# Moved steps around the latent statistics and the turned query, and attention steps that alternate between two heads

## The reference, cut to what matters

```python
h = rms_norm(x, g_pre_mix) * (1 + sc1) + sh1
proj = h @ w_in                       # q latent 384, kv latent 256, rope key 32, lru x 1024, lru gate 1024, merge 2048
q = rms_norm(q_lat, g_q) @ w_q_up     # 8 heads of 64 + 32 (the 32 are rotated for the latent tokens)
ckv = rms_norm(kv_lat, g_kv);  kv = concat(ckv, cache) @ w_kv_up          # per head 64 of k, 64 of v
y_mla = softmax(q k^T * scale) v @ w_o_mla
xc = centred_conv(lru_x);  r, i = sigmoid(xc @ w_rg), sigmoid(xc @ w_ig)  # in 8 blocks, two directions
h_t = a_t * h_(t-1) + sqrt(1 - a_t^2) * i_t * xc_t                        # a scan forward, a scan backward
y_lru = (hf + hb) * gelu(lru_gate) @ w_o_lru
y = (sigmoid(merge1) * y_mla + sigmoid(merge2) * y_lru) @ w_out
x = x + g1 * rms_norm(y);  then a SwiGLU feed-forward block, modulated and normed in the same way
```

## Time and profile before

| | us |
|---|---|
| median of 3 runs | 1445.06 (1444.82 to 1445.11) |
| the profiled execution | 1440.7 |
| its span, first instruction to last | 1438.9 |
| PE busy | 1342.7 (93%) |
| DVE busy | 736.9 (51%) |
| ACT busy | 664.9 (46%) |
| DMA queue's share of 16 engines | 41.5% |

### The profile page before, as it was taken

The page is one execution under the profiler, slowest core; times in us unless marked ns, Lnnn a source line. Parts: engine busy times, 40 slices in busy tenths (PEclk is TensorE's granted clock), DMA queues, the critical chain, the costliest instruction groups (busy, mean ns, idle before and its releaser), DMA issues.

```text
span 1438.9 us, 20857 instructions
## 1 busy us (share of the span) xinstructions
PE 1342.7 (93%) x8171; PEld 1216.5 (85%) x8171; DVE 736.9 (51%) x1306; ACT 664.9 (46%) x1199; POOL 19.2 (1%) x38
## 2 busy tenths in 40 slices
PE   5999879889999999999999988897999999999998
PEld 4888879867878999998789987896878799999886
DVE  2777474454566333343368764735536554434423
ACT  3478763544346333333255877435533533323422
POOL 0000000200000000000000000002000000000000
PEclk9999989999999999999999999998999999999999
DMA  9443534322154555555225434351232243445522
GB/s 342 148 136 121 176 119 151 116 103 87 32 190 136 176 175 162 169 170 176 91 86 163 140 116 147 117 195 59 88 103 103 77 133 118 132 148 180 200 92 84
DMA packets 135061, 196.27 MB, mean 136 GB/s; under 512 B 9730, under 2 KB 68268, under 8 KB 134964
## 3 DMA queue, kind: packets, MB, share of 16 engines
q1 hardware_dynamic: 134964, 194.94, 41.5%
HBM read 193.03 MB, written 1.88 MB: 135 GB/s over the span
## 4 chain that ended last, share of the span: by engine, by line
PE 77%; DVE 9%; ACT 8%; DMA 3%; issue 2%; SPq 0%; DVEq 0%; ACTq 0%
PE bank L638 15%; PE bank L645 15%; PE bank L646 15%; PE bank L724 6%; PE bank L723 6%; PE bank L725 6%; PE bank L677 3%; DVE weight_low L1461 2%; ACT weight_high L1092 2%; PE bank L1026 2%; PE bank L601 1%; PE bank L1004 1%; DMA raw<-in_w_in 1%; PE bank L705 1%; PE bank L853 1%
## 5 line engine op out<-in xcount | busy, mean ns | idle before, releaser
L645 PE MATMUL bank<-act_low,weight_high 128*128 128x384 f32 x1440 | 492.8, 342 | 5.1 <-DVE weight_low L1461 4.3
L646 PE MATMUL bank<-act_high,weight_low 128*128 128x384 f32 x1440 | 487.7, 339 | 0.0
L1461 DVE TENSOR_TENSOR weight_low<-raw,weight_high 128x1024 fp32r<-128x1024 f32 (+5 forms) x282 | 319.0, 1153 | 277.1 <-ACT weight_high L1092 276.6
L1092 ACT ACTIVATE weight_high<-raw 128x1024 fp32r<-128x1024 f32 (+5 forms) x282 | 273.4, 995 | 317.0 <-DMA raw<-in_w_ffn_in 86.3
L638 PE MATMUL bank<-act_high,weight_high 128*128 128x384 f32 x1440 | 325.3, 347 | 18.9 <-ACT lru_tau L1268 12.2
L645 PEld LDWEIGHTS bank<-act_low,weight_high 128*128 128x128 f32 x1440 | 275.5, 191 | 14.4 <-DVE weight_low L1461 6.8
L638 PEld LDWEIGHTS bank<-act_high,weight_high 128*128 128x128 f32 x1440 | 257.0, 192 | 31.4 <-ACT lru_tau L1268 12.8
L646 PEld LDWEIGHTS bank<-act_high,weight_low 128*128 128x128 f32 x1440 | 275.0, 191 | 0.0
L723 PE MATMUL bank<-weight_high,hid_high 128*128 128x512 f32 x264 | 104.4, 395 | 0.0
L725 PE MATMUL bank<-weight_high,hid_low 128*128 128x512 f32 x264 | 102.8, 389 | 0.0
L724 PE MATMUL bank<-weight_low,hid_high 128*128 128x512 f32 x264 | 102.8, 389 | 0.0
(11 more groups left out here) (221 smaller groups left out, 1526.8 us busy)
## 6 DMA issues: line engine op xcount, KB each, us to landing
raw<-in_w_ffn_in SPq DMA_DIRECT2D x176, 256.0 KB, 4.0
mod_weight<-in_w_mod SPq DMA_DIRECT2D x80, 512.0 KB, 4.8
raw<-in_w_in SPq DMA_DIRECT2D x72, 512.0 KB, 4.2
raw<-in_w_ffn_out SPq DMA_DIRECT2D x44, 512.0 KB, 4.1
first_mod<-in_w_mod SPq DMA_DIRECT2D x4, 2048.0 KB, 14.3
raw<-in_w_o_lru SPq DMA_DIRECT2D x16, 512.0 KB, 3.6
raw<-in_w_out SPq DMA_DIRECT2D x16, 512.0 KB, 3.4
raw<-in_w_o_mla SPq DMA_DIRECT2D x8, 512.0 KB, 6.0
```

Of the source, the lines that this page charges most:

```text
L645: nc.tensor.matmul(o, view[0][:, kk, cols], low[:, k, :], start=False, stop=False)
L646: ins = nc.tensor.matmul(o, view[1][:, kk, cols], high[:, k, :], start=False, stop=k == total - 1)
L1092: nc.scalar.activation(high, w, ACT.Copy).then_inc(*AC.step())
L1461: nc.vector.tensor_tensor(low, w, high.bitcast(F), ALU.subtract).then_inc(*VE.step())
```

## The change

Four groups of edits. (1) DVE copies lx1's banks before convolutions 2 and 3. (2) In m2a and m2b: ACT does GELUs 0 to 3 ahead of the weight halves of m2a 1 and 2, and all halves up to m2b 3 one load sooner; the inverse roots come after place 5 in place of 2; DVE makes the low halves one load sooner, and mod_result(6) ahead of the scans. (3) PE rotates the first four heads before kn and the others after it (`rotate`), DVE's rotation is `turn_query`, in two places among the lru products and with `sq[j]` as its scratch, mod_partial(4) comes after lru product 1, and the halves of qn1 1 and ol0 0 come sooner. (4) `head_tile` gives the head and tile of a step: within six steps they go (head 0, q 0), (head 1, q 0), (0, 1), (1, 1), (0, 2), (1, 2). Value products are issued at even steps for the two steps before, tile by tile in turn between the heads, whose outputs are the two halves of the columns; a step's last increment stands for both.

```diff
+        def head_tile(s):
+            return 2 * (s // 6) + s % 2, s % 6 // 2
...
+                def rotate(j):
+                    pe.wait_ge(*at(AC, "qn", 3 * j + 2))
+                    if j == 1:
+                        pe.wait_ge(*at(VE, "turned_query", 0))
+                    nc.tensor.matmul(bank("qn1", 3)[:, TS * j:TS * j + TS], rot[:, :], sq[2 + j][:, TP:T], start=True, stop=True
+                                     ).then_inc(*PE.step("qrot", j))
+                rotate(0)
                 loads = of_job("kv")
                 banks_free("kn")
...
-                for j in range(2):
-                    pe.wait_ge(*at(AC, "qn", 3 * j + 2))
-                    nc.tensor.matmul(bank("qn1", 3)[:, TS * j:TS * j + TS], rot[:, :], sq[2 + j][:, TP:T], start=True, stop=True
-                                     ).then_inc(*PE.step("qrot", j))
+                    if k == KC - 1:
+                        rotate(1)
...
                 def values(s):
-                    h, q = divmod(s, 3)
-                    tiles = (0,) if q == 0 else (1, 2, 3)
-                    if h % 2 == 0 and h >= 2 and q == 0:
-                        pe.wait_ge(*at(VE, "o_low", h // 2 - 1))
-                    pe.wait_ge(*at(AC, "pt", s))
...
+                    tiles = (0,) if head_tile(s)[1] == 0 else (1, 2, 3)
+                    if s % 6 == 0 and s > 0:
+                        pe.wait_ge(*at(VE, "o_low", s // 6 - 1))
+                    pe.wait_ge(*at(AC, "pt", s + 1))
                     for j, k in enumerate(tiles):
...
+                        for e in (s, s + 1):
+                            h, q = head_tile(e)
+                            half = slice(64 * (h % 2), 64 * (h % 2) + 64)
+                            ins = nc.tensor.matmul(bank("attn", 3)[half, q * P:q * P + P], vv[:, k, h * VD:h * VD + VD],
+                                                   sq[2 + e % 2][:, j * P:j * P + P], start=j == 0, stop=j == len(tiles) - 1)
+                    ins.then_inc(*PE.step("values", s + 1))
+                    PE.also("values", s)
...
-                    if s >= 1:
-                        values(s - 1)
+                    if s >= 2 and s % 2 == 0:
+                        values(s - 2)
...
-                        if b == 1 and e == 2:
+                        if b == 1 and e == 5:
                             ac.wait_ge(*at(PE, "stq", QC + KC - 1))
...
-                highs("m2a", 1)
-                for c in range(C):
...
+                for c in range(4):
+                    ac.wait_ge(*at(AC, "gate_input", c))
+                    nc.scalar.activation(ybuf[:, c, :], ybuf[:, c, :], ACT.Gelu_apprx_tanh).then_inc(*AC.step("gelu", c))
+                highs("m2a", 2)
+                for c in range(4, C):
...
-                lru_coefficients(1, {1: ("m2a", 2), 3: ("m2a", 3), 5: ("m2b", 0), 7: ("m2b", 1), 9: ("m2b", 2)})
+                lru_coefficients(1, {1: ("m2a", 3), 3: ("m2b", 0), 5: ("m2b", 1), 7: ("m2b", 2), 9: ("m2b", 3)})
...
+                branch_inputs(1)
                 convolve(2)
                 convolve(3)
-                branch_inputs(1)
...
-                lows("m2a", 1)
+                lows("m2a", 2)
                 squared_roots(4)
                 mod_partial(7)
-                lows("m2a", 2)
+                lows("m2a", 3)
                 squared_roots(5)
+                mod_result(6)
                 scans(4, 0)
-                lows("m2a", 3)
+                lows("m2b", 0)
                 squared_roots(6)
-                lows("m2b", 0)
+                lows("m2b", 1)
                 scans(5, 1)
                 squared_roots(7)
-                lows("m2b", 1)
-
-                mod_result(6)
+                lows("m2b", 2)
...
+                    if c == 1:
+                        mod_partial(4)
+                        lows("kv", 0)
+                    if c == 6:
+                        turn_query(0)
                     if c >= 1:
                         lru_low(c - 1)
                     if c == 2:
                         lows("kv", 1)
-                        mod_partial(4)
+                turn_query(1)
                 lru_low(C - 1)
                 lows("ol0", 0)
```

More of the change, by code:

```diff
@@ L991, in scores @@
                 def scores(s):
-                    h, q = divmod(s, 3)
+                    h, q = head_tile(s)
                     if s >= 2:
@@ L1007, in turn @@
                 def turn(s):
-                    n = 1 if s % 3 == 0 else 3
+                    n = 1 if head_tile(s)[1] == 0 else 3
                     if s >= 1:
@@ L1053, in _ @@
                 split_job("ol1", hh, hl, between=attention_steps(13))
-                values(23)
+                values(22)
                 split_job("om0", oh, ol, ready=(VE, "o_low"), ready_high=(AC, "o_high"))
@@ L1296, in _ @@
                 lru_gates(1, (("gg1", 2), ("gates1", 1), ("gg1", 3), ("m2a", 0)))
-                highs("m2a", 1)
-                for c in range(C):
[L1299 to L1304, removed]
-                lru_coefficients(1, {1: ("m2a", 2), 3: ("m2a", 3), 5: ("m2b", 0), 7: ("m2b", 1), 9: ("m2b", 2)})
+                for c in range(4):
[3 more added lines that the diff above has]
+                for c in range(4, C):
+                    ac.wait_ge(*at(PE, "gg1", c % 4))
+                    nc.scalar.activation(ybuf[:, c, :], bank("gg1", c % 4)[:, 0:T], ACT.Gelu_apprx_tanh).then_inc(*AC.step("gelu", c))
+                lru_coefficients(1, {1: ("m2a", 3), 3: ("m2b", 0), 5: ("m2b", 1), 7: ("m2b", 2), 9: ("m2b", 3)})
                 def merge(job, dst, c0, label):
@@ L1334, in _ @@
                 nc.scalar.activation(out_h[:, :], bank("outs", 2)[0:2 * C, 0:P], ACT.Copy).then_inc(*AC.step("outs"))
-                highs("qn1", 0)
+                highs("qn1", 1)
                 merge("m1b", m1, 4, "m1")
@@ L1360, in _ @@
                 for g in range(4):
+                    if g == 2:
+                        highs("ol0", 0)
                     if g == 3:
@@ L1367, in _ @@
                     AC.also("kn", g)
-                highs("ol0", 0)
                 for g in range(4):
@@ L1769, in _ @@
                                                    in1=sq[1][:, :], op0=ALU.mult, op1=ALU.mult).then_inc(*VE.step("ckv_full", k))
-                lows("m2b", 2)
                 scans(6, 2)
@@ L1827, in _ @@
                 ve.wait_ge(*at(PE, "m1b", 3))
-                lows("kv", 0)
                 def lru_low(c):
@@ L1834, in lru_low, with turn_query @@
                                             ).then_inc(*VE.step("lru_low", c))
+                def turn_query(j):
+                    ve.wait_ge(*at(PE, "qrot", j))
+                    turned = sq[j]
+                    nc.vector.tensor_tensor(turned[:, 0:TS], bank("qn1", 3)[:, TS * j:TS * j + TS], sin[:, :], ALU.mult
+                                            ).then_inc(*VE.step("turned_query", j))
+                    nc.vector.tensor_tensor(sq[2 + j][:, TP:T], sq[2 + j][:, TP:T], cos[:, :], ALU.mult).then_inc(*VE.step())
+                    own()
+                    for e in range(4):
+                        quad = slice(32 * e, 32 * e + 32)
+                        nc.vector.tensor_tensor(qt(4 * j + e)[TURNED, TP:T], sq[2 + j][quad, TP:T], turned[quad, 0:TS], ALU.add
+                                                ).then_inc(*VE.step("qrot", 4 * j + e))
                 for c in range(C):
@@ L1842, in _ @@
                         lows("kv", 1)
-                        mod_partial(4)
+                turn_query(1)
                 lru_low(C - 1)
                 lows("ol0", 0)
-                for j in range(2):
-                    ve.wait_ge(*at(PE, "qrot", 1))
-                    own()
-                    nc.vector.tensor_tensor(t[j][:, 0:TS], bank("qn1", 3)[:, TS * j:TS * j + TS], sin[:, :], ALU.mult).then_inc(*VE.step())
-                    nc.vector.tensor_tensor(sq[2 + j][:, TP:T], sq[2 + j][:, TP:T], cos[:, :], ALU.mult).then_inc(*VE.step())
-                    own()
-                    for e in range(4):
-                        quad = slice(32 * e, 32 * e + 32)
-                        nc.vector.tensor_tensor(qt(4 * j + e)[TURNED, TP:T], sq[2 + j][quad, TP:T], t[j][quad, 0:TS], ALU.add
-                                                ).then_inc(*VE.step("qrot", 4 * j + e))
                 def mix_lru(b):
```

12 lines of the change are left out of this document (3 added, 9 removed).

## The result

The changed kernel takes 1372.46 us (median of 4 runs, 1369.37 to 1374.85), the kernel before in the same batch 1444.94 (4 runs, 1439.73 to 1445.11): a ratio of 0.9505, 95% interval 0.9476 to 0.9535, or 72 us less.

A forecast was written before the change was run, and what follows sets the result against it. TensorE, busy 93% of the span, bounds the kernel; its waits cost themselves plus half clock behind them. 4.7 + 2 x (11.3 + 13.4 + 4.0) = 62.1 us off the 1445.06 median gives 1383.0, range 1370 to 1407.

The forecast's parts named there:

- The forecast case: Whole kernel: all parts save 62.1 us together, giving a median of 1383.0 us; chance 0.58.
- the rivals: Halves don't overlap, 1389 us (0.16); scans take over in the latents, 1394 us (0.2); slower than before, 1455 us (0.02).
- Copies of lx: Before two convolutions, layer 0 only: PE's 3.0 us wait and 1.7 us of half clock go, 4.7 us once.
- Latents: m2a and m2b: earlier statistics, low halves and mod_result(6) shorten PE's waits, 11.3 us per layer, 7 to 13.
- the wait for the statistics: m2a, PE before L878, waiting for mod_partial(7): shrinks from 3.7 to 2.1 us, saving 1.6 us.
- the last low half's: Low half of m2b 3, still behind scans(6,2) on DVE: a late wait of about 1.1 us.
- "qn1" and the turned query: PE's waits of 4.5 and 5.9 us before L940 and L977 go with their half clock: 13.4 us per layer, 11 to 14.
- Values side by side: Attention: two heads' value products overlap in column halves, records 17.2 to 8.7 us, net gain 4.0 us per layer.
- what I took back: Attention, off the 8.7 us: 0.9 at the end, 0.9 at step 12, 0.9 at the output weight's load, 2.0 for o_high and even copies.
- The rule about row groups: Value products: by this rule the halves wouldn't overlap, attention gains 0.9 us, total 1389 us; chance 0.16.
- The scans taking over: Rival in m2a and m2b: chain through squared_roots(6) 4 to 6 us longer, part gives 6, total 1394 us; chance 0.2.
- All of om and the FFN is unchanged: Sign after attention: output products and feed-forward part keep their time, a saving of 0.

The follow-up runs named there:

- p1: Kernel before with only lx1's bank copies moved ahead of convolutions 2 and 3: 1438.63 us, ratio 0.9982.
- e8: Changed kernel with mod_result(6) put back behind the low halves on DVE: 1388.64 us, ratio 0.9624.
- e7: Changed kernel with ACT's inverse roots of the latents back at the third pair: 1380.06 us, ratio 0.9566.
- p4: Kernel before with only the attention edits, steps alternating between two heads and value products in turn: 1433.45 us, ratio 0.9943.
- e5: The changed kernel run again, unaltered, beside its variants on one chip: 1373.41 us, ratio 0.9514 to the kernel before.
- e10: Changed kernel with DVE's four mix products of the first chunk behind step 13 in place of step 12: 1367.93 us, ratio 0.9492.
- e11: Changed kernel with a modulation weight's quarters 2 and 3 loaded behind the output weight's second load, not ahead of its first: 1364.58 us, ratio 0.9454.
- e9: Changed kernel with both heads' value products in the lower half of the columns, head by head: 1375.94 us, ratio 0.9539.

## Why the prediction held, point by point

The forecast case came, with 1372.46 us against 1383.0 and a range of 1370 to 1407. None of the rivals did. The size was 10.5 us off. Of that, 6.6 lie in which executions are compared (last paragraph of this section): the profiled ones saved 65.9 us, and my sum for them was 62.1. That the two are so close is luck in part, since the parts are off by up to 5 us in both directions.

- **Copies of lx, 4.7 us: right** where it arises. The lead in p1 is 4.8 at the statistics; in the total of p1 it is 2.9, and how much of it arrives there stays open.
- **Latents, 11.3 per layer: too low.** 14.2 in layer 0 (18.9 less 4.7), 16.6 in layer 1. Mechanism and order were right: e8 shows that mod_result(6) waited for its place alone. Three terms were mis-sized: the wait for the statistics is 1.12, not 2.1; the last low half's is 0.44, not 1.1; and the clock stays at 1.00 behind both, where "I leave the half clock behind it as it is" kept 1.7 us. I named 13 as what the part gives if that goes too; it went. The later inverse roots, which I had only said would save ACT a wait, are worth 6.7 us (e7).
- **"qn1" and the turned query, 13.4 per layer: right in layer 0**, 14.7 to the first score, of which 1.1 comes back at the first softmax, as the prediction had it. Layer 1 gave 16.1, or 15.0 after the softmax, above my 14: behind "qn1" the kernel before has 6.8 us of half clock there, 3.4 in layer 0, and I had taken layer 1 for a copy.
- **Values side by side: the records right, what they give in the whole too high.** They were to fall from 17.2 to 8.7 us and fell to 8.8 in p4 and 9.4 in the whole, where one group of twelve lies at half clock. Alone the part gave what I had said, 8.0 us. In the whole change 7.8 us of records gave 1.4 and 1.0 us of time (2.5 in layer 0 with the 1.1 just named), and 2.2 and 2.1 in e5, not 4.0. The step that failed is the sum of what I took back, 4.7 us. Its terms can be held against the same waits of PE in the kernel before:
```profile
338.66 0.30 PE L1013 MATMUL bank<-ident,sq 128*128 128x128 f32 x1 [0.56 <-DVE sq L1870]
356.36 0.91 PE L1004 MATMUL bank<-keys,q_last 96*128 96x384 f32 x2 [1.23 <-ACT sq L1395]
357.88 0.52 PE L1013 MATMUL bank<-ident,sq 128*128 128x128 f32 x3 [0.61 <-DVE sq L1870]
```
  Around the mix products 0.56 us has become 2.20 (0.92 + 1.28): 1.6 more, where I took back 0.9; e10 removed only the 1.28, so the 0.92 may belong to the 2.0. At the output weight's load 1.84 has become 2.88 (1.85 + 1.03): 1.0 for 0.9, and e11 shows what that wait is. At the end 0.6 for 0.9. Of the 2.0 for o_high and for the even copies nothing else shows: these growths and that of the first softmax (0.21 to 1.54) already make 4.6 of the 4.7 us by which PE's idle time grew, 3.8 to 8.5. So the waits took back 3.3 us, less than I had booked. What I put at nothing without a word is the clock: I priced no half clock in attention, and the whole change has 6.8 us of it in the layer; PE is busy for 66.9 us there where 73.0 less 8.4, the records at full clock, is 64.6. Of the 5.1 us that records less waits would leave (8.4 less 3.3), this clock takes 2.3 and the first softmax 1.3, and 1.4 is the measured rest.
- **The rule about row groups** (the Trainium skill, "TensorE: Matmul & The Clock Gate", Part 3) has a weight load pass running matmuls only where its row group differs, and I took from it that halves with all 128 rows wouldn't overlap. They do: e9 has both heads in the same half at 1.52 us, the changed kernel has them in two at 0.88, so here column halves alone were enough. The tiles of 32 columns had foretold it. The same Part also lists packing by columns alone as a gain, 2.38 times for three tiles, which I had passed over.
- **The scans taking over:** they don't, and e7 shows how near they are: 1.6 us of wait on ACT is all it takes.
- **"All of om and the FFN is unchanged":** wrong in time though not in work. PE's two waits before the feed-forward part are the same 0.59 and 2.28 us in both kernels. In layer 0 the kernel before has its full clock behind them:
```profile
434.00:445.00 11.00, 8.13 (x56) 7.50 (x55) 7.33 (x14) 7.79 (x20) 0.00 (x0) 1.00 0.00 0
736.00:750.00 14.00, 11.13 (x71) 10.15 (x70) 8.99 (x17) 10.25 (x28) 0.00 (x0) 1.00 0.13 37
```
  the changed one half of it, at 405.5 and 709.3 (above). In layer 1 it is the other way round: half clock for 6.8 us in the kernel before and for 3.4 in the changed one. So the 4.1 us lost and the 1.3 won in these rows, whose instructions are the same, are no effect of the edits that these runs could show.

The 66 us between two spans and the 72 between medians differ because the runs of one kernel differ: the profiled execution of before was 4.2 us under the median that it is compared with, that of the changed kernel 2.4 over its own.

## What to carry to other kernels

Where PE waits, look for the short instruction that ends just before it goes on and ask what it queued behind: one addition of 0.16 us was worth 15 us of time. Before you shorten PE's work in a stretch, find the transfers that land in it and where they stand in their queue; a faster PE meets a late load sooner, and moving that load (e11, 8.8 us) gave more than the shorter records did in the whole change (2.4 by the marks, 4.3 in e5). And weigh an edit in the finished order, not alone: the values gave 8.0 us by themselves and less than that in the whole, and the table load, moved early, made the wait longer that it was to end.

## What the runs showed of the hardware

- Two matmuls with all 128 rows, in different halves of 64 columns and in the same bank, run side by side: 12 records in 0.88 us in turn, 1.15 when all of one half is issued first, 1.52 in one half.
- The granted clock after a wait isn't a matter of that wait alone. The same 2.28 us with the same work around it is followed by none, 3.4 or 6.8 us at half clock, and this differs from layer to layer within one execution (kernel before: none at 439.7, 6.8 at 1144.9). And e9 kept 1.00 through attention of layer 0 with 6.9 us idle where the changed kernel fell twice. Four runs of the changed kernel went from 1369.37 us at a mean clock of 0.988 to 1374.85 at 0.985. A gain of a few us therefore can't be read from one profile, and what decides where the clock falls stays open.
